# Both head rows' diagonal and level products of the gated linear attention in one slot, alternating row by row

## What is computed

```
log_a = log_sigmoid(gk_lr @ w_gk_up + b_gk) / 16
S_t = diag(exp(log_a_t)) S_{t-1} + k_t^T v_t ;  o_t = q_t S_t          # GLA, 4 heads
attn[i,j] = sum_d q[i,d] k[j,d] exp(b[i,d] - b[j,d]),  j <= i          # b: running sum of log_a
o_g = rmsnorm(attn @ v) * silu(g_g)
o_m = softmax(q k^T / 8 + bias, causal) @ v                            # MoBA with one block, 8 heads
out = concat(o_g, o_m) @ W_out
```

## Time and profile before

| | |
|---|---|
| median of 3 runs | 559.12 us (558.36 to 559.14) |
| span of the profiled execution | 556.7 us |
| TensorE busy | 547.1 us, 98% |
| VectorE busy | 312.4 us, 56% |
| ScalarE busy | 272.8 us, 49% |
| DMA, mean | 177 GB/s |

### The profile page before, as it was taken

The page is one execution under the profiler, slowest core; times in us unless marked ns, Lnnn a source line. Parts: engine busy times, 40 slices in busy tenths (PEclk is TensorE's granted clock), DMA queues, the critical chain, the costliest instruction groups (busy, mean ns, idle before and its releaser), DMA issues.

```text
span 556.7 us, 6914 instructions
## 1 busy us (share of the span) xinstructions
PE 547.1 (98%) x2583; PEld 443.5 (80%) x2583; DVE 312.4 (56%) x375; ACT 272.8 (49%) x333; POOL 11.9 (2%) x24
## 2 busy tenths in 40 slices
PE   8999999999999999999999999999999999999994
PEld 4888888888788888877878888888888888888883
DVE  4575555555535464347787585555554554353575
ACT  5964443535334456864153666353534443343646
POOL 1400000000000010000000000000000000000000
PEclk9999999999999999999999999999999999999998
DMA  8997565654685665440346087565565646536202
GB/s 283 337 349 237 156 210 162 206 170 152 208 252 183 214 229 183 151 151 1 111 127 211 8 262 240 160 191 186 179 197 166 210 122 215 163 105 226 77 1 75
DMA packets 72550, 98.37 MB, mean 177 GB/s; under 512 B 3377, under 2 KB 48641, under 8 KB 72401
## 3 DMA queue, kind: packets, MB, share of 16 engines
q1 hardware_dynamic: 71104, 93.34, 52.5%
q0 software_dynamic: 1264, 4.68, 2.7%
q10 hardware_dynamic: 160, 0.07, 0.0%
HBM read 97.01 MB, written 2.63 MB: 179 GB/s over the span
## 4 chain that ended last, share of the span: by engine, by line
PE 98%; DMA 1%; ACT 0%; issue 0%; DVE 0%; DVEq 0%
PE acc L482 87%; PE side L482 5%; PE turn L524 4%; DMA h<-in_x 1%; PE turn L482 1%; ACT L1067 0%; DVE res L1410 0%; DVEq L200 0%; PE side L524 0%; ACT rtmp L1072 0%; ACT spare L1067 0%; ACT junk L1054 0%; DVE rstd L1408 0%; ACT gate L1047 0%; DVEq L1407 0%
## 5 line engine op out<-in xcount | busy, mean ns | idle before, releaser
L1097 DVE TENSOR_TENSOR w_lo<-raw,w_hi 128x2048 fp32r<-128x2048 f32 (+1 forms) x89 | 197.4, 2219 | 109.0 <-ACT w_hi L835 108.8
L482 PE MATMUL acc<-w_hi,hT_hi 128*128 128x512 f32 x496 | 197.9, 399 | 0.0
L835 ACT ACTIVATE w_hi<-raw 128x2048 fp32r<-128x2048 f32 (+1 forms) x89 | 165.0, 1856 | 62.5 <-PE acc L482 59.7
L482 PE MATMUL acc<-w_hi,hT_lo 128*128 128x512 f32 x496 | 193.6, 390 | 0.0
L482 PE MATMUL acc<-w_lo,hT_hi 128*128 128x512 f32 x496 | 193.1, 389 | 0.0
L482 PEld LDWEIGHTS acc<-w_hi,hT_hi 128*128 128x128 f32 x496 | 93.2, 188 | 20.3 <-issue 1.7
L482 PEld LDWEIGHTS acc<-w_hi,hT_lo 128*128 128x128 f32 x496 | 93.1, 188 | 20.0
L482 PEld LDWEIGHTS acc<-w_lo,hT_hi 128*128 128x128 f32 x496 | 93.3, 188 | 17.9
L482 PE MATMUL acc<-w_hi,a_hiT 128*128 128x512 f32 x176 | 70.1, 398 | 0.0
L482 PE MATMUL acc<-w_hi,a_loT 128*128 128x512 f32 x176 | 69.6, 395 | 0.0
L482 PE MATMUL acc<-w_lo,a_hiT 128*128 128x512 f32 x176 | 69.6, 395 | 0.0
(11 more groups left out here) (165 smaller groups left out, 314.5 us busy)
## 6 DMA issues: line engine op xcount, KB each, us to landing
raw<-in_ffn_w_gu SPq DMA_DIRECT2D x86, 512.0 KB, 4.8
raw<-in_ffn_w_down SPq DMA_DIRECT2D x40, 512.0 KB, 4.7
raw<-in_w_in SPq DMA_DIRECT2D x24, 512.0 KB, 4.5
raw<-in_w_out SPq DMA_DIRECT2D x8, 512.0 KB, 4.4
raw<-in_w_ple_gate SPq DMA_DIRECT2D x8, 512.0 KB, 4.7
raw<-in_ffn_w_down SPq DMA_DIRECT2D x8, 256.0 KB, 3.1
bias_skew_dram<-bias_row_dram POOLq DMA_DIRECT2D x1, 1536.0 KB, 8.2
h<-in_x SPq DMA_DIRECT2D x2, 512.0 KB, 5.3
```

What stands on the lines that cost most here:

```text
L482: return nc.tensor.matmul(o, lhsT, rhs, start=start, stop=stop, skip_group_check=True)
L835: A(w_hi[:, slot, :nk * N], raw[:, slot, :nk * N], ACT.Copy).then_inc(hi_ready, 1)
L1097: V.tensor_tensor(w_lo[:, slot, :nk * N], raw[:, slot, :nk * N], w_hi[:, slot, :nk * N].bitcast(F32), ALU.subtract).then_inc(lo_ready, 1)
```

## The change

`diag` and each `lv` become one piece for both head rows. The piece opens both side banks at once and then issues, for each block k, the matmul of partitions 0-63 into the first bank and that of partitions 64-127 into the second. The number, shapes and operands of the matmuls are the same, and so is the order of the side banks' uses. In `MIX`, fourteen places between units 41 and 44 become twelve between 41 and 45; `pv0`, `pv1` and `pv2` stand alone now, and `lv3` comes one tick later, after (45, 0). In `DVE_STEPS` the halves of `lv1` are read together, after `pt1.0` and `pt1.1`, and `lo46` comes after `pt2.0` and `pt2.1`. ScalarE's order and the DMA queues are as before.

```diff
@@ MIX
     (41, 0): ["sc1.0", "sc1.1"],
-    (41, 1): ["diag.0"],
-    (41, 2): ["diag.1"],
-    (41, 3): ["lv0.0"],
-    (42, 0): ["lv0.1"],
-    (42, 1): ["pv0", "lv1.0"],
+    (41, 2): ["diag"],
+    (42, 0): ["lv0"],
+    (42, 1): ["pv0"],
     (42, 2): ["pt1.0", "pt1.1"],
-    (42, 3): ["lv1.1"],
-    (43, 0): ["sc2.0", "sc2.1"],
-    (43, 1): ["pv1", "lv2.0"],
-    (43, 2): ["lv2.1"],
-    (44, 0): ["pt2.0", "pt2.1"],
-    (44, 1): ["sc3.0", "sc3.1"],
-    (44, 2): ["pv2", "lv3.0"],
-    (44, 3): ["lv3.1"],
+    (42, 3): ["lv1"],
+    (43, 1): ["sc2.0", "sc2.1"],
+    (43, 2): ["pv1"],
+    (44, 0): ["lv2"],
+    (44, 1): ["pt2.0", "pt2.1"],
+    (44, 2): ["sc3.0", "sc3.1"],
+    (44, 3): ["pv2"],
+    (45, 0): ["lv3"],
     (45, 1): ["pt3.0", "pt3.1"],
@@ DVE_STEPS
-... "lv0", "pv0", "lv1.0", "pt1.0", "pt1.1", "lo44", "lv1.1", "Z2", ... "Z3", "lo46", "pt2.0", "pt2.1", "sc3", ...
+... "lv0", "pv0", "pt1.0", "pt1.1", "lv1", "lo44", "Z2", ... "Z3", "pt2.0", "pt2.1", "lo46", "sc3", ...
@@ the matrix engine's step, diag (lv is alike)
-                    hh = int(s[5])
-                    o = side_open(s)
+                    o = [side_open(f"diag.{hh}") for hh in range(2)]
                     pe.wait_ge(turn_act, turned("T_g1"))
-                    r = slice(64 * hh, 64 * hh + 64)
                     for k in range(4):
                         c = slice(k * P, (k + 1) * P)
-                        ins = mm(o[:, c], k_gT[r, c], q_gT[r, c], True, True)
-                    ins.then_inc(side_done, 1)
+                        for hh in range(2):
+                            r = slice(64 * hh, 64 * hh + 64)
+                            ins = mm(o[hh][:, c], k_gT[r, c], q_gT[r, c], True, True)
+                            if k == 3:
+                                ins.then_inc(side_done, 1)
```

More of the change, by code:

```diff
@@ L167, in plan_side @@
                 uses.append((s, "act"))
+            elif s == "diag" or s[:2] == "lv":
+                uses += [(f"{s}.{hh}", "dve") for hh in range(2)]
             elif s[:2] not in ("T_", "pt") and (s[:2] != "pv" or s[:3] == "pvg"):
@@ L702, in step @@
                     ins.then_inc(turn_done, 1)
-                elif s[:4] == "diag":
-                    hh = int(s[5])
-                    o = side_open(s)
+                elif s == "diag":
+                    o = [side_open(f"diag.{hh}") for hh in range(2)]
                     pe.wait_ge(turn_act, turned("T_g1"))
-                    r = slice(64 * hh, 64 * hh + 64)
                     for k in range(4):
                         c = slice(k * P, (k + 1) * P)
-                        ins = mm(o[:, c], k_gT[r, c], q_gT[r, c], True, True)
-                    ins.then_inc(side_done, 1)
+                        for hh in range(2):
[3 more added lines that the diff above has]
+                                ins.then_inc(side_done, 1)
                 elif s[:2] == "lv":
-                    hh = int(s[4])
-                    o = side_open(s)
-                    r = slice(64 * hh, 64 * hh + 64)
+                    o = [side_open(f"{s}.{hh}") for hh in range(2)]
                     pe.wait_ge(Z_ready, 2 * int(s[2]) + 2)
@@ L720, in step @@
                         w = 1 << lv
[L721 to L731, removed]
+                        for k in range(2 if lv == 7 else 4):
+                            for hh in range(2):
+                                r = slice(64 * hh, 64 * hh + 64)
+                                if lv == 7:
+                                    c = k * T
+                                    ins = mm(o[hh][:, T + k * P:T + (k + 1) * P], E[r, 0, c:c + P],
+                                             E[r, 8, c + P:c + T], True, True)
+                                else:
+                                    z = E[r, lv + 1, k * P:(k + 1) * P]
+                                    ins = mm(o[hh][:, a * T + k * 64:a * T + (k + 1) * 64], z,
+                                             view(z, [[2 * w, 64 // w], [1, w]], w), True, True)
+                                if a == 1 and k == (1 if lv == 7 else 3):
+                                    ins.then_inc(side_done, 1)
                 elif s[:3] == "T_o":
```

## The result

| | before | changed |
|---|---|---|
| median | 558.87 us (558.36 to 559.14, 4 runs) | 551.55 us (551.21 to 551.95, 4 runs) |
| span of the profiled execution | 556.7 us | 549.9 us |
| TensorE busy | 547.1 us | 539.6 us |

The ratio is 0.9866, with a 95% interval from 0.9854 to 0.9879: 1.3% faster, 7.3 us by the medians. The forecast was 551.7. The profiled spans differ by less, 6.8 us: the changed kernel's TensorE is 0.50 us later already at sc1 (252.83 against 252.33), from the first 12 us of the kernel, which the change doesn't touch. Lengths within the stretch are free of that.

A forecast was written before the change was run, and what follows sets the result against it. TensorE was taken as the bound. Savings of 7.6 us from paired passes plus 0.7 and 0.4 of fixed parts make 8.7; less 1.3 of stalls, 7.4, so 559.1 becomes 551.7 us, range 550.0 to 554.0.

The forecast's parts named there:

- What bounds the kernel: From the last tick ahead of sc1 to pt3, TensorE is busy for all 50.67 us, VectorE for 40.01.
- Price of a pass: In diag and the levels, each matmul pass costs TensorE about 0.112 us, the pace of the weight loads.
- Full pairing: In the merged diag and lv pieces, passes on partitions 0-63 and 64-127 run together, two in 0.112 us.
- rival 3: The merged pieces don't overlap at all; only switches are saved, 1.1 us, giving 558.0 us; chance 3%.
- The sum: TensorE's saving in diag and lv0 to lv3: 7.6 us of passes, 0.7 and 0.4 of fixed parts, 8.7 us.
- Waits: TensorE stalls for VectorE's reading of banks: 0.9 us at pt1, 0.2 at pt3 and 0.2 at pvg0.
- The walk: TensorE and VectorE followed step by step from diag to pt3 with profiled durations, giving 1.3 us of stalls.
- `lo46` "helps": Moving lo46 behind the pt2 copies lets them end at 286.4 instead of 288.6, ahead of pv2's turn at 288.2.
- Outside the stretch: Nothing changes outside the stretch from the last tick ahead of sc1 to pt3; DMA has room for earlier loads.
- Rival 1: VectorE becomes the bound between sc1 and pt3, with 3.5 to 5 us of stalls: 554 to 555.5 us; chance 8%.
- Rival 2: Passes in merged pieces start in strict program order, four taking 0.25 us, not 0.224: 552.6 us; chance 7%.
- Rival 4: Each of 63 changes of half in merged pieces exposes a weight load, 0.10 us each: slower, 564.3 us; chance 3%.

## Why the prediction was right, point by point

- **What bounds the kernel.** TensorE, as rows 1 and 2 said: what it was spared arrived in full, less the waits.
- **Price of a pass, 0.112 us; blocks of 1.09, 1.93 and 1.53.** The merged blocks took 1.09 (256.65 to 257.74), 1.93 and 1.54. The other half is free. The pairing alone is worth 7.6 us of pieces, as the kernel on one half shows.
- **Full pairing, from `sc`.** Right for this change, but for a narrower reason than I gave. I wrote in rival 3 that looking ahead "has a shorter way here"; I had not seen that it has a limit at all, about 4 passes, and that the alternation, or at least blocks as short as `sc`'s, is what the gain hangs on. The changed kernel's blocks of 2 passes are shorter than `sc`'s of 4, so the reading was safe here; the same reading, carried to head-by-head blocks, would have been wrong (558.58 us).
- **The sum, 8.7 us.** The window shrank by 7.69 with 1.35 of waits up to pt3's end; of these the 1.03 at pt1 lies in the window, so 8.7 were spared.
- **Waits, 0.9 + 0.2 + 0.2 = 1.3.** Measured 1.03 at pt1, 0.32 at pt3, 0.07 at pvg0 (its block took 0.88 instead of 0.81), 1.4 in all, and at the places named. The walk missed some 0.1 per handover. Ahead of lv3 there was no wait, as worked out.
- **`lo46` "helps".** It removed the gap at pv2 as I wrote, but not the time: without it the gaps behind shrink by as much. The walk stopped one wait too early there.
- **Outside the stretch.** Nothing that the change made: the median fell by 7.3 and the sum had 7.4. In the profiles, from pt3 on, TensorE's work is 0.39 us longer, which is the waits at pt3 and pvg0.
- **Rival 1 (VectorE)** fell with the two kernels in which a later pt1 and another order of VectorE's steps brought 1.2 and 0.4 us by the medians.
- **Rival 2 (strict order)**: a level took 1.93, not the 2.1 that its own price gives (8 fours of 0.25 and 0.14; the prediction wrote 2.2). Its page, the Trainium skill's "TensorE: Matmul & The Clock Gate", Part 3, says that matmuls start in program order. The trace of the changed kernel disagrees: diag's second half starts some 0.01 us behind the first, ahead of the first half's second pass, which comes before it in the program. With head blocks the second half started beside the first half's 13th pass of 16, with three more of the first half still to come. So there is such freedom, but only a few passes of it. The prediction's sentence that the Trainium skill's rule on weight loads agrees with rows 5 goes too far. The two halves' loads do overlap there, but diag.0's loads, all on one half, start every 0.11 us while each pass of that half lasts 0.27, so loads run beside passes of their own half as well. No term of the sum rested on that.
- **Rivals 3 and 4**: not met by this change. Rival 3's price was off, though: I put no overlap at 558.0, and measured it at 562.88. The term that I left out is the clock, which fell around pieces of 3.7 us with passes on one half and cost 6.3 us there. Rival 4 had a slower kernel for another reason, a load laid bare at each change of half. A level of 1.93 us with 15 changes leaves no room for it; what a change costs where nothing overlaps was not tested.

## What to carry to other kernels

Small float32 products on partitions 0-63 and on 64-127 ran at the price of one here, each half with a bank of its own, as long as the instruction stream changed half at least every four passes (two float32 matmuls). Both halves into one bank was not tried. When such a gain makes TensorE faster, walk the other engines' order once with the measured durations: the waits came out within 0.13 us each at the places named, and moving one piece by a tick (pt1) or two steps of VectorE's order to a later place (lo47 and lo48) got them back. Where several waits hang on one run of another engine's work, as at pv2, pt3 and pvg0, another order within that run only moves the wait; it goes when work leaves the run.

## What the runs showed of the hardware that I had not expected

- The looking ahead across halves reaches about 4 passes. A level of 32 passes took 1.93, 1.98, 2.55 and 3.32 us with blocks of 2, 4, 8 and 16 passes, and 3.71 on one half alone.
- In the profiled executions the granted clock fell from 2.4 to 1.2 GHz behind a piece of 3.3 us (one of three) and behind or within each of three of 3.7 us, though TensorE was busy all the time. In all of these pieces most passes ran alone on 64 partitions with 64 columns each. It did not fall behind such pieces of 1.9 us with ticks between (the kernel before), nor behind 2.5 us in blocks of 8 passes, nor behind 1.9 us of paired ones. At the lower level an `acc` matmul costs 0.43 us instead of 0.23. Whether the partitions, the columns or the length do it was not told apart.
- Passes side by side did not slow each other: 0.112 us per pair, as per single one.
